# Attention over padded 128x128 tiles, products with queries on partitions, scaling moved to the eviction, long and short blocks in turn

## The chip, the cores and the metric

One Trainium2 chip, one core. The metric is the device time of one execution in microseconds (us), the median of the runs. TensorE (PE) multiplies, its weight loads are listed apart as PEld; VectorE is DVE, ScalarE is ACT, GpSimd is POOL, SyncE (SP) issues DMAs.

## What is computed

The whole program runs two recurrent mixer layers over 1024 tokens and then one transformer block. The change touches the attention of that block: for each of 8 query blocks of 128 tokens, a sliding-window attention with sinks (8 heads, 2 key-value heads) and a latent attention over the keys that an index picked (8 heads, keys and values the same 128 latent numbers). 16 meta tokens stand ahead of all others.

```
s  = einsum('bnqhgd,bnkhd->bnhgqk', qb, kw) * (64 ** -0.5) + bias      # window: own and previous block
pr = e / (e.sum(-1) + exp(sink - m));   o_a = einsum('bnhgqk,bnkhd->bnqhgd', pr, vw)
...
s  = einsum('bqhc,bqkc->bqhk', qa, c_sel) * scale + bias               # latent: selected keys only
pr = softmax(s);   lat = einsum('bqhk,bqkc->bqhc', pr, c_sel);   o_b = einsum('bphc,chd->bphd', lat, w_uv)
...
mixed = gate_a * (o_a @ w_branch_a) + gate_b * (o_b @ w_branch_b)
```

All data is float32. The profile shows two PE passes for such a product and one for a transpose.

## The kernel before, around the change

There is no scheduler. Each engine runs its own program, written out by hand, and waits on counters; `attend_order` is the one list that all engines follow in the attention, each doing its share of a step and skipping the rest. Query block i (0 to 7) has N = 144 + 128 i keys, in i + 2 key tiles: one of the 16 meta keys, the others of 128.

One step s_ carries a head k = s_ of the latent attention through a pipeline. PE does, in this order: `scores(s_)` (N columns, in pieces of at most 512), `latent(s_-3)` (probabilities times latents, a product for each key tile), `turn_p(s_-2)` (a transpose for each key tile, up to four to a bank), `raised(s_-4)` (latent result times w_uv). Between them DVE scales, masks and finds the row maximum (`scores`), ACT takes the exponentials (`expo`) and copies every PSUM result to SBUF, and POOL multiplies the exponentials by one over their sum (`scale`, line 2589), which `turn_p` waits for. Before, k runs through blocks 0, 0, ... 7, 7, eight heads each.

The window attention has 32 pieces m = s_ // 2 (block m // 4, a head of each key-value head). In an even step PE does `swa_scores(m)` and `swa_turn(m-1)`, in an odd step `swa_values(m-1)`. DVE and ACT make the softmax, POOL scales it (line 2583), and ACT copies the turned window, the event `pa` (line 1616), after the exponentials of `swa_scores(m)` (lines 1606 and 1607), as the list has them in that order. Every block also needs `queries` and `absorbed` (lines 1079 and 1089), two products that make the absorbed queries of its eight heads.

PE takes its PSUM banks in turn from rings, and waits until the bank's former tenant has been copied out. Nearly everything small shares one ring of two banks, 7 and 2:

```
swa_s, mla_s, mla_p, small_b = Ring([0], True), Ring([3, 4]), Ring([5, 6]), Ring([7, 2])
```

`small_b` serves `swa_turn`, `swa_values`, `queries`, `absorbed`, `latent` and `raised`. The PE lines of the profile are 1047 `swa_scores`, 1057 and 1058 `swa_turn`, 1069 and 1070 `swa_values`, 1079 `queries`, 1089 `absorbed`, 1097 `scores`, 1105 `turn_p`, 1113 `latent`, 1121 `raised`. When all is copied out (`attn_done`), SP issues the loads of the next stage.

## Time and profile before

| | us |
|---|---|
| time before, median of 3 runs | 3779.39 (3776.23 to 3781.73) |
| the profiled execution, its time | 3773.92 |
| its span | 3772.2 |
| PE busy in the span | 3529.2 (94%) |
| the attention stage, first transfer of PE work to last | 2417.6 to 2789.2 |
| in it: PE, DVE, ACT, POOL busy (2418 to 2794) | 356.1, 195.3, 212.7, 169.0 |

PE is busy 94% of the span, and 82% of the chain that ended last lies on it. The attention is a tenth of the span. A busy PE counts pipelined matmuls to their modelled ends, so the start of one group to the start of the next is the better measure of what it takes; the granted clock of a stretch (1.00 is 2.4 GHz, 0.50 is 1.2 GHz) stands in the tables by stretches. The profiled execution is 5.5 us under the median of the runs.

### The profile page before, as it was taken

The numbers are of one execution on the slowest core, as the hardware profiler recorded it, in microseconds if no ns is written. First come the engines' busy times: TensorE is split into PE (matmuls) and PEld (weight loads), VectorE is DVE, ScalarE is ACT, GpSimd is POOL, SyncE is SP. The second block draws the span as 40 slices with busy tenths as digits, with TensorE's granted clock in tenths as the row PEclk, the third lists the DMA queues.
The fourth block names the chain that finished last, engine by engine and source line by source line (L and its number), as shares of the span: only waits on it lengthen the run. The fifth ranks groups of instructions, "written<-read, shape, count | busy, mean of one in ns | idle before, by whom it ended". The sixth has DMA issues, their size and how long they took to land.

```text
span 3772.2 us, 46285 instructions
## 1 busy us (share of the span) xinstructions
PE 3529.2 (94%) x19030; PEld 2511.3 (67%) x19030; DVE 1698.5 (45%) x3307; ACT 1109.3 (29%) x2310; POOL 615.2 (16%) x872
## 2 busy tenths in 40 slices
PE   8889999989999899999878899899999999999997
PEld 7775876777677577577453344467754478888886
DVE  3433444344343435435417889656532232332424
ACT  3432442243244334133212111256531121111112
POOL 0210120011021423012511011235520000000000
PEclk9899999999999999999978999889999999999999
DMA  3010110110001011011010021100030011111111
GB/s 132 23 35 12 40 41 1 40 29 24 28 29 41 12 37 34 23 46 71 1 70 34 22 78 59 64 1 1 1 140 34 12 56 45 45 56 45 56 45 45
DMA packets 36527, 151.54 MB, mean 40 GB/s; under 512 B 4983, under 2 KB 9785, under 8 KB 28890
## 3 DMA queue, kind: packets, MB, share of 16 engines
q1 hardware_dynamic: 36314, 148.57, 11.4%
q8 instruction: 150, 2.46, 0.3%
q14 instruction: 63, 0.52, 0.0%
HBM read 132.82 MB, written 15.73 MB: 39 GB/s over the span
## 4 chain that ended last, share of the span: by engine, by line
PE 82%; DVE 7%; ACT 4%; POOL 3%; issue 2%; DMA 1%; SPq 0%; POOLq 0%; DVEq 0%; ACTq 0%
PE pp L540 7%; PE pp L541 7%; PE pp L542 7%; PE pp L1176 6%; PE pp L1178 6%; PE pp L1177 6%; PE pp L1026 6%; PE pp L706 5%; PE pp L1158 3%; PE pp L1113 2%; PE pp L1142 2%; PE pp L851 2%; PE pp L1016 2%; PE pp L1097 1%; PE pp L1002 1%
## 5 line engine op out<-in xcount | busy, mean ns | idle before, releaser
L540 PE MATMUL pp<-gx_hi,pw_hi 128*128 128x512 f32 x1168 | 485.9, 416 | 28.6 <-DVE pw_lo L1755 27.7
L541 PE MATMUL pp<-gx_lo,pw_hi 128*128 128x512 f32 x1168 | 466.1, 399 | 0.0
L542 PE MATMUL pp<-gx_hi,pw_lo 128*128 128x512 f32 x1168 | 465.9, 399 | 0.0
L540 PEld LDWEIGHTS pp<-gx_hi,pw_hi 128*128 128x128 f32 x1168 | 226.2, 194 | 77.1 <-DVE pw_lo L1755 30.5
L1176 PE MATMUL pp<-x_hi,wt_hi 128*128 128x512 f32 x704 | 274.7, 390 | 1.1 <-DVE x_lo L2289 1.1
L1178 PE MATMUL pp<-x_hi,wt_lo 128*128 128x512 f32 x704 | 274.2, 390 | 0.0
L1177 PE MATMUL pp<-x_lo,wt_hi 128*128 128x512 f32 x704 | 274.2, 389 | 0.0
L542 PEld LDWEIGHTS pp<-gx_hi,pw_lo 128*128 128x128 f32 x1168 | 225.3, 193 | 49.7
L541 PEld LDWEIGHTS pp<-gx_lo,pw_hi 128*128 128x128 f32 x1168 | 226.4, 194 | 43.6
L706 PE MATMUL pp<-xT,arena 128*128 128x512 f32 x512 | 233.8, 594 | 6.3 <-DVE arena L1929 6.3
L1755 DVE TENSOR_TENSOR pw_lo<-arena,pw_hi 128x1024 fp32r<-128x1024 f32 x73 | 89.5, 1228 | 242.0 <-ACT pw_hi L1231 241.9
L2331 DVE TENSOR_TENSOR arena<-arena,pp 128x1024 f32<-128x1024 f32 x22 | 26.9, 1222 | 375.0 <-ACT arena L1732 375.0
L1732 ACT ACTIVATE arena<-pp 128x1024 f32<-128x1024 f32 x22 | 22.6, 1029 | 556.8 <-PE pp L1178 556.8
L2188 DVE MAX8 small<-w 128x8 f32<-128x656 f32 (+6 forms) x180 | 167.1, 928 | 2.8
L2190 DVE MATCH_REPLACE8 w<-small,w 128x656 f32<-128x656 f32 (+6 forms) x180 | 164.4, 914 | 0.0
L2602 POOL TENSOR_SCALAR small<-small 128x1 f32<-128x1 f32 x16 | 3.0, 190 | 973.0 <-ACT arena L1687 973.0
L706 PEld LDWEIGHTS pp<-xT,arena 128*128 128x128 f32 x512 | 94.8, 191 | 94.1 <-issue 83.1
L1176 PEld LDWEIGHTS pp<-x_hi,wt_hi 128*128 128x128 f32 x704 | 132.2, 188 | 28.8 <-DVE x_lo L2289 1.4
L1177 PEld LDWEIGHTS pp<-x_lo,wt_hi 128*128 128x128 f32 x704 | 132.2, 188 | 27.6 <-issue 0.2
L1178 PEld LDWEIGHTS pp<-x_hi,wt_lo 128*128 128x128 f32 x704 | 132.2, 188 | 27.4
L1176 PE MATMUL pp<-wt_hi,a_hi 128*128 128x512 f32 x352 | 139.6, 397 | 4.7 <-DVE a_lo L2333 4.7
L2318 DVE TENSOR_TENSOR y<-y,pp 128x512 f32<-128x512 f32 x176 | 115.9, 685 | 60.6 <-PE pp L1178 60.0
(391 smaller groups left out, 6735.6 us busy)
## 6 DMA issues: line engine op xcount, KB each, us to landing
arena<-in_tiles_dram SPq DMA_DIRECT2D x73, 512.0 KB, 3.6
arena<-in_units_dram SPq DMA_DIRECT2D x33, 1024.0 KB, 4.9
xT<-in_w_outs_dram SPq DMA_DIRECT2D x6, 2048.0 KB, 8.4
xT<-in_wall_dram SPq DMA_DIRECT2D x6, 2048.0 KB, 8.2
w<-in_wall_dram SPq DMA_DIRECT2D x4, 2048.0 KB, 8.1
gates_scratch<-arena SPq DMA_DIRECT2D x32, 256.0 KB, 2.4
arena<-gates_scratch SPq DMA_DIRECT2D x8, 1024.0 KB, 4.9
arena<-in_xT_dram SPq DMA_DIRECT2D x8, 512.0 KB, 8.0
```

The lines of the kernel that those rows point to most:

```text
L540: mm(b[:, hs], wh[:, c], X[0][:, k, hs], k == 0, False)
L541: mm(b[:, hs], wh[:, c], X[1][:, k, hs], False, False)
L542: m = mm(b[:, hs], wl[:, c], X[0][:, k, hs], False, k == 7)
L706: m = mm(b, oT[:, t * 128:(t + 1) * 128], wo[:, t * 1024 + hf * 512:t * 1024 + hf * 512 + 512], t == 0, t == 3)
L1026: m = mm(b, xT[:, k, n * 128:(n + 1) * 128], ws[:, k * 512:(k + 1) * 512], k == 0, k == 7)
L1158: m = mm(b, mixT[n % 2][:, k * 128:(k + 1) * 128], wt[:, (k % 4) * 1024 + hf * 512:(k % 4) * 1024 + hf * 512 + 512], k == 0, k == 7)
L1176: mm(o, l[0][:, c], r[0][:, d], first, False)
L1177: mm(o, l[0][:, c], r[1][:, d], False, False)
L1178: return mm(o, l[1][:, c], r[0][:, d], False, last)
L2188: e.max(m8, wk[:, 0:N]).then_inc(*did("m8", i, r_))
L2190: e.match_replace(out=wk[:, 0:N], in_to_replace=m8, in_values=wk[:, 0:N], imm_value=MARK).then_inc(*did("mr", i, r_))
L2318: tt(yv, yv, at("dn", j, n, hf), ALU.add).then_inc(*did("yd", j, n, hf))
```

## The change

1. The tile of meta keys is padded: rows 16 to 127 of the values `ckv[:, 0, :]` and `av[:, 0, :]` are zero, and the first key tile is transposed, copied and multiplied as one of 128 (its other columns meet zeros). ACT's separate copy of 16 rows (line 1652) becomes part of the following one.
2. `raised` and `swa_values` have their operands exchanged: the result has queries on partitions, 64 columns wide, with the full array and 64 moving columns. So it is turned afterwards, several heads at a time: `turn_o` (two transposes for four heads of a latent block) and `swa_out` (two transposes for two window pieces), both in `small_b`.
3. Nothing is scaled on POOL. ACT multiplies by one over the sum when it copies `raised`, DVE when it copies `swa_values` (which ACT did before).
4. Blocks come in pairs: k even is a head of blocks 7, 6, 5, 4, k odd one of 0, 1, 2, 3. Both blocks' `queries` and `absorbed` of the first pair stand ahead of step 0, the later ones in steps 8, 9, 13 and 14 of 16. There is a third buffer for absorbed queries. The window's pieces keep their order.

```diff
-        qab = [a.rearrange("p (h c) -> p h c", h=8) for a in (room(1024), masks[:, :, :].rearrange("p l c -> p (l c)"))]
+        qab = [a.rearrange("p (h c) -> p h c", h=8) for a in (room(1024), masks[:, :, :].rearrange("p l c -> p (l c)"), room(1024))]
...
+        obq = [room(256), room(256)]
+        oaq = consts[:, 128:384]
...
+        def blk(q):
+            return q // 2 if q % 2 else 7 - q // 2
+
+        def step_of(i, hd):
+            return 16 * min(i, 7 - i) + 2 * hd + (i < 4)
+
+        def last_step(q):
+            return step_of(blk(q), 7)
+
         def keys(k):
-            i = k // 8
-            tiles = [(0, 0, 16)] + [(t_, 16 + 128 * (t_ - 1), 128) for t_ in range(1, i + 2)]
-            return (i, k % 8, Sb[k % 3], 144 + 128 * i, tiles, slice(i * 128, (i + 1) * 128))
-
-        def attend_order(queries, absorbed, scale, scores, latent, turn_p, raised, expo, swa_scores, swa_turn, swa_scale,
-                         swa_values):
-            queries(0)
-            absorbed(0)
-            for s_ in range(68):
+            q = k // 16 * 2 + k % 2
+            i = blk(q)
+            tiles = [(0, 0)] + [(t_, 16 + 128 * (t_ - 1)) for t_ in range(1, i + 2)]
+            return (i, k // 2 % 8, Sb[k % 3], 144 + 128 * i, tiles, slice(i * 128, (i + 1) * 128), qab[q % 3])
+
+        def attend_order(queries, absorbed, scale, scores, latent, turn_p, raised, turn_o, expo, swa_scores, swa_turn, swa_scale,
+                         swa_values, swa_out):
+            for q in range(2):
+                queries(q)
+                absorbed(q)
+            for s_ in range(69):
                 if 1 <= s_ < 65:
                     scale(s_ - 1)
                 if s_ < 64:
...
                     latent(s_ - 3)
                 if 2 <= s_ < 66:
                     turn_p(s_ - 2)
-                if s_ >= 4:
+                if 4 <= s_ < 68:
                     raised(s_ - 4)
+                if s_ >= 5 and (s_ - 5) // 2 % 4 == 3:
+                    turn_o(s_ - 5)
                 if s_ < 64:
                     expo(s_)
                 m = s_ // 2
...
                         swa_scores(m)
                     if 1 <= m < 33:
                         swa_turn(m - 1)
+                    if 3 <= m < 34 and m % 2:
+                        swa_out(m - 2)
                 else:
                     if m < 32:
                         swa_scale(m)
                     if 1 <= m < 33:
                         swa_values(m - 1)
-                i = s_ // 8 + 1
-                if i < 8 and s_ % 8 == 3:
-                    queries(i)
-                if i < 8 and s_ % 8 == 5:
-                    absorbed(i)
+                for later, at_ in ((2, 8), (3, 13)):
+                    q = s_ // 16 * 2 + later
+                    if q < 8 and s_ % 16 == at_:
+                        queries(q)
+                    if q < 8 and s_ % 16 == at_ + 1:
+                        absorbed(q)
...
-        attn_done = [("sv", 31), ("ra", 63), ("oa", 31), ("ob", 63), ("P", 63), ("sp", 31)]
+        attn_done = [("ot", 63), ("ao", 31), ("oT", 63), ("aT", 31), ("oa", 31)]
...
             def swa_values(m):
                 i, j, d, cs, k0, ln, bo = swa_keys(m)
                 pa = PA[d].rearrange("p (q t c) -> p q t c", q=2, t=2)
-                first = 128 if i else 16
                 b = place_(small_b, ("sv", m), ("oa", m))
                 pe.wait_ge(("pa", m))
                 for p in range(2):
                     r = slice(64 * p, 64 * p + 64)
-                    mm(b[r, 0:128], av[0:first, i, r], pa[0:first, p, 0, :], True, False)
-                    q = mm(b[r, 0:128], av[:, i + 1, r], pa[:, p, 1, :], False, True)
+                    for t_ in range(2):
+                        q = mm(b[:, r], pa[:, p, t_, :], av[:, i + t_, r], t_ == 0, t_ == 1)
                 q.then_inc(*did("sv", m))
 
+            def swa_out(m):
+                b = place_(small_b, ("ao", m), ("aT", m))
+                pe.wait_ge(("oa", m - 1), ("oa", m))
+                for t_ in range(2):
+                    q = tr(b[:, t_ * 128:(t_ + 1) * 128], oaq[:, t_ * 128:(t_ + 1) * 128], ident)
+                q.then_inc(*did("ao", m))
...
             def turn_p(k):
-                pe.wait_ge(("P", k))
+                pe.wait_ge(("x", k))
                 for q0 in range(0, len(some), 4):
                     b = place_(mla_p, ("tp", k, q0), ("pt", k, q0))
-                    for x_, (t_, a, c) in enumerate(some[q0:q0 + 4]):
-                        q = tr(b[0:c, x_ * 128:(x_ + 1) * 128], s_[:, a:a + c], ident)
+                    for x_, (t_, a) in enumerate(some[q0:q0 + 4]):
+                        q = tr(b[:, x_ * 128:(x_ + 1) * 128], s_[:, a:a + 128], ident)
                     q.then_inc(*did("tp", k, q0))
 
             def latent(k):
-                i, hd, s_, N, some, cs = keys(k)
+                i, hd, s_, N, some, cs, qa = keys(k)
                 b = place_(small_b, ("la", k), ("lat", k))
                 pe.wait_ge([("pt", k, q0) for q0 in range(0, len(some), 4)])
-                for t_, a, c in some:
-                    q = mm(b[:, 0:128], ckv[0:c, t_, :], PT[k % 2][0:c, t_, :], t_ == 0, t_ == i + 1)
+                for t_, a in some:
+                    q = mm(b[:, 0:128], ckv[:, t_, :], PT[k % 2][:, t_, :], t_ == 0, t_ == i + 1)
                 q.then_inc(*did("la", k))
 
             def raised(k):
-                i, hd, s_, N, some, cs = keys(k)
+                i, hd, s_, N, some, cs, qa = keys(k)
                 b = place_(small_b, ("ra", k), ("ob", k))
-                r = slice(64 * (k % 2), 64 * (k % 2) + 64)
                 pe.wait_ge(("lat", k))
-                mm(b[r, 0:128], wuv[:, hd * 64:(hd + 1) * 64], lat[k % 2], True, True).then_inc(*did("ra", k))
+                mm(b[:, 0:64], lat[k % 2], wuv[:, hd * 64:(hd + 1) * 64], True, True).then_inc(*did("ra", k))
+
+            def turn_o(k):
+                b = place_(small_b, ("ot", k), ("oT", k))
+                pe.wait_ge(("ob", k))
+                for t_ in range(2):
+                    q = tr(b[:, t_ * 128:(t_ + 1) * 128], obq[k % 2][:, t_ * 128:(t_ + 1) * 128], ident)
+                q.then_inc(*did("ot", k))
...
-                if i:
-                    act(PA[d], b, ACT.Copy).then_inc(*did("pa", m))
-                else:
-                    act(pa[0:16, :, 0, :], bb_[0:16, :, 0, :], ACT.Copy)
-                    act(pa[:, :, 1, :], bb_[:, :, 1, :], ACT.Copy).then_inc(*did("pa", m))
-
-            def swa_values(m):
+                act(PA[d], b, ACT.Copy).then_inc(*did("pa", m))
+
+            def swa_out(m):
                 i, j, d, cs, k0, ln, bo = swa_keys(m)
-                ac.wait_ge(("sv", m))
-                act(oaT[:, j, cs], at("sv", m)[:, 0:128], ACT.Copy).then_inc(*did("oa", m))
+                ac.wait_ge(("ao", m))
+                act(oaT[:, j - 1:j + 1, cs], at("ao", m)[:, 0:256].rearrange("p (t c) -> p t c", t=2), ACT.Copy
+                    ).then_inc(*did("aT", m))
...
                 for q0 in range(0, len(some), 4):
                     part = some[q0:q0 + 4]
                     b = at("tp", k, q0)
                     ac.wait_ge(("tp", k, q0))
-                    lo = 0
-                    if part[0][2] == 16:
-                        i_ = act(pt[0:16, 0, :], b[0:16, 0:128], ACT.Copy)
-                        lo = 1
-                    if lo < len(part):
-                        i_ = act(pt[:, q0 + lo:q0 + len(part), :].rearrange("p t q -> p (t q)"), b[:, lo * 128:len(part) * 128],
-                                 ACT.Copy)
-                    i_.then_inc(*did("pt", k, q0))
+                    act(pt[:, q0:q0 + len(part), :].rearrange("p t q -> p (t q)"), b[:, 0:len(part) * 128], ACT.Copy
+                        ).then_inc(*did("pt", k, q0))
 
...
             def raised(k):
-                r = slice(64 * (k % 2), 64 * (k % 2) + 64)
-                ac.wait_ge(("ra", k))
-                act(obT[r, hd // 2, cs], at("ra", k)[r, 0:128], ACT.Copy).then_inc(*did("ob", k))
+                ac.wait_ge(("ra", k), ("rd", k), ("ot", k - 2) if hd % 4 == 0 and k >= 2 else None)
+                act(obq[k % 2][:, hd % 4 * 64:hd % 4 * 64 + 64], at("ra", k)[:, 0:64], ACT.Copy, scale=mla_t[k % 6][2]
+                    ).then_inc(*did("ob", k))
+
+            def turn_o(k):
+                i, hd, s_, N, some, cs, qa = keys(k)
+                ac.wait_ge(("ot", k))
+                act(obT[:, hd // 4 * 2:hd // 4 * 2 + 2, cs], at("ot", k)[:, 0:256].rearrange("p (t c) -> p t c", t=2), ACT.Copy
+                    ).then_inc(*did("oT", k))
...
+            def swa_values(m):
+                j, rd = m % 4, swa_t[m % 2][5]
+                o = oaq[:, j % 2 * 128:j % 2 * 128 + 128]
+                dv.wait_ge(("sv", m), ("srd", m), ("ao", m // 2 * 2 - 1) if m >= 2 else None)
+                tt(o.rearrange("p (q c) -> p q c", q=2), at("sv", m)[:, 0:128].rearrange("p (q c) -> p q c", q=2),
+                   rd.unsqueeze(2).to_broadcast([128, 2, 64]), ALU.mult).then_inc(*did("oa", m))
...
+            e.memset(ckv[:, 0, :], 0.0)
+            e.memset(av[:, 0, :], 0.0).then_inc(*did("zpad"))
...
-            def swa_scale(m):
-                i, j, d, cs, k0, ln, bo = swa_keys(m)
-                rd = swa_t[d][5]
-                po.wait_ge(("srd", m))
-                for p in range(2):
-                    i_ = ts(sS[d][:, p, 0:ln], sS[d][:, p, 0:ln], rd[:, p:p + 1], None, ALU.mult)
-                i_.then_inc(*did("sp", m))
-
-            def scale(k):
-                i, hd, s_, N, some, cs = keys(k)
-                po.wait_ge(("rd", k))
-                ts(s_[:, 0:N], s_[:, 0:N], mla_t[k % 3][2], None, ALU.mult).then_inc(*did("P", k))
```

How PE's order moves is shown at two places. The first is an even step and the start of the odd one after it, in the middle of a sweep: PE before, from the window's scores in step 10 on (pp1 holds banks 2 and 3, pp3 banks 6 and 7; for `latent`, `raised`, the window's turn and values, pp3 is bank 7 and pp1 bank 2).

```order
L1047 MATMUL pp0<-arena 128x256 x2
L1057 MATMUL pp3<-consts,w2 128x128
L1058 MATMUL pp3<-consts,w2 128x128
L1057 MATMUL pp3<-consts,w2 128x128
L1058 MATMUL pp3<-consts,w2 128x128
L1097 MATMUL pp2<-arena,masks 128x272
L1113 MATMUL pp1<-arena 128x128 x3
L1105 MATMUL pp3<-consts,arena 16x128
L1105 MATMUL pp3<-consts,arena 128x128 x2
L1121 MATMUL pp3<-w3,xT 64x128
L1069 MATMUL pp1<-w2,arena 64x128
L1070 MATMUL pp1<-w2,arena 64x128
```

And PE now, from the window's scores in step 6 on (lines of the changed kernel: 1066 window scores, 1076 and 1077 window turn, 1095 `swa_out`, 1124 scores, 1140 `latent`, 1132 `turn_p`, 1147 `raised`, 1088 window values):

```order
L1066 MATMUL pp0<-arena 128x144 x2
L1076 MATMUL pp1<-consts,arena 128x128
L1077 MATMUL pp1<-consts,arena 128x128
L1076 MATMUL pp1<-consts,arena 128x128
L1077 MATMUL pp1<-consts,arena 128x128
L1095 MATMUL pp3<-consts 128x128 x2
L1124 MATMUL pp2<-arena,masks 128x144
L1140 MATMUL pp1<-arena 128x128 x9
L1132 MATMUL pp3<-consts,arena 128x128 x2
L1147 MATMUL pp3<-xT,w3 128x64
L1088 MATMUL pp1<-arena,w2 128x64 x4
```

Before, the bank of the window's turn (pp3) came back for `raised` (L1121), behind scores, `latent` and `turn_p`. Now, where `swa_out` stands behind the turn (m odd), that bank (pp1) comes back for `latent` (L1140), behind `swa_out` and the short block's scores alone. Where m is even there is no L1095, and the bank still comes back for `raised`.

The second place is the start of the stage on PE, before:

```order
L1079 MATMUL pp3<-arena,xT 128x128 x8
L1089 MATMUL pp1<-arena,xT 128x128 x4
L1089 MATMUL pp3<-arena,xT 128x128 x4
L1097 MATMUL pp1<-arena,w2 128x144
L1047 MATMUL pp0<-arena 128x144 x2
```

and now (1105 `queries`, 1115 `absorbed`):

```order
L1105 MATMUL pp3<-arena,xT 128x128 x8
L1115 MATMUL pp1<-arena,xT 128x128 x4
L1115 MATMUL pp3<-arena,xT 128x128 x4
L1105 MATMUL pp1<-arena,xT 128x128 x8
L1115 MATMUL pp3<-arena,xT 128x128 x4
L1115 MATMUL pp1<-arena,xT 128x128 x4
L1124 MATMUL pp1<-arena,w2 128x512
```

A second pair of `queries` and `absorbed` moved ahead of the first scores, and those are now of block 7.

## Rows read from the trace of the kernel before

**Rows 1.** The page: its first line.

```profile
span 3772.2 us, 46285 instructions
```

**Rows 2.** Stretches: length, busy PE, PEld, DVE, ACT, POOL, clock, DMA share, GB/s.

```profile
2424.30:2444.80 20.50, 18.55 (x71) 13.09 (x72) 8.80 (x35) 9.07 (x35) 5.21 (x8) 0.50 0.00 0
2448.20:2468.70 20.50, 20.50 (x76) 13.01 (x74) 6.39 (x21) 7.49 (x29) 3.19 (x5) 0.50 0.00 0
2478.90:2768.30 289.40, 275.81 (x1814) 198.50 (x1812) 169.38 (x436) 175.23 (x553) 147.31 (x104) 1.00 0.00 1
```

**Rows 3.** Timeline of PE, blocks 1 and 2: start, us, line, count, idle before.

```profile
2496.97 0.70 PE L1047 MATMUL pp<-arena 64*128 64x256 f32 x4
...
2498.65 1.12 PE L1113 MATMUL pp<-arena 16*128 16x128 f32 x6
2499.61 0.49 PE L1105 MATMUL pp<-consts,w 128*16 128x128 f32 x3
2501.35 0.43 PE L1121 MATMUL pp<-w,xT 128*64 128x128 f32 x2 [1.25 <-ACT w L1616]
...
2504.77 0.70 PE L1047 MATMUL pp<-arena 64*128 64x256 f32 x4
```

**Rows 4.** Timeline of DVE and ACT in the same pair of steps.

```profile
2497.72 0.69 DVE L2216 SCALAR_TENSOR_TENSOR w<-pp,arena 128x512 f32<-128x512 f32 x1 [0.95 <-PE pp L1047]
...
2499.63 0.51 ACT L1606 ACTIVATE w<-w,small 128x256 f32<-128x256 f32 x1 [1.73 <-DVE small L2224]
...
2500.73 0.57 ACT L1616 ACTIVATE w<-pp 128x512 f32<-128x512 f32 x1
```

**Rows 5.** Timeline of PE, block 4, two steps.

```profile
2595.02 0.32 PE L1121 MATMUL pp<-w,xT 128*64 128x128 f32 x1
...
2596.16 2.05 PE L1079 MATMUL pp<-arena,xT 128*128 128x128 f32 x16 [0.27 <-ACT xT L1667]
2598.05 1.27 PE L1097 MATMUL pp<-arena,w 128*128 128x512 f32 x4
2599.25 1.80 PE L1113 MATMUL pp<-arena 16*128 16x128 f32 x12
2600.88 0.82 PE L1105 MATMUL pp<-consts,w 128*16 128x128 f32 x6
2601.63 0.43 PE L1121 MATMUL pp<-w,xT 128*64 128x128 f32 x2
2601.99 0.49 PE L1047 MATMUL pp<-arena 64*128 64x256 f32 x2
```

**Rows 6.** Timeline of PE: block 7; last, an earlier stage.

```profile
2765.74 1.04 PE L1105 MATMUL pp<-consts,w 128*16 128x128 f32 x8
2767.07 0.33 PE L1105 MATMUL pp<-consts,w 128*128 128x128 f32 x1 [0.29 <-ACT arena L1655]
...
67.93 1.84 PE L566 MATMUL pp<-consts,arena 128*128 128x1 f32 x16
```

**Rows 7.** Stretches of the stage before, and a PE row of its timeline.

```profile
2076.20:2079.60 3.40, 1.25 (x6) 0.48 (x5) 0.88 (x2) 2.09 (x9) 0.02 (x1) 1.00 0.00 0
2079.60:2086.40 6.80, 6.80 (x9) 2.89 (x10) 5.96 (x12) 0.73 (x2) 1.47 (x4) 0.50 0.00 0
...
2093.13 1.18 PE L965 MATMUL pp<-arena 64*128 64x272 f32 x2 [2.15 <-DVE w L2166]
```

**Rows 8.** Timeline of PE, the start of the stage.

```profile
2417.59 3.62 PE L1079 MATMUL pp<-arena,xT 128*128 128x128 f32 x16 [5.65 <-DMA gates_scratch<-arena]
...
2424.37 0.85 PE L1097 MATMUL pp<-arena,w 128*128 128x144 f32 x2 [0.69 <-ACT w L1633]
```

**Rows 9.** Groups by shape in the attention; last, a piece of the chain behind.

```profile
L1652 ACT ACTIVATE arena<-pp 16x128 f32<-16x128 f32 x64 | 16.8, 262 | 7.7 <-PE pp L1105 6.5
...
L1105 PE MATMUL pp<-consts,w 128*16 128x128 f32 x43 | 12.3, 286 | 1.5 <-POOL w L2589 1.5
...
2793.14 25.43 DMA arena<-gates_scratch
```

More of the change, by code:

```diff
@@ L353, in program @@
         swa_t = [tuple(sm(2) for _ in range(6)) for _ in range(2)]
-        mla_t = [tuple(sm(1) for _ in range(3)) for _ in range(3)]
+        mla_t = [tuple(sm(1) for _ in range(3)) for _ in range(6)]
         def skewed(a):
@@ L1080, in queries, with absorbed @@
                                bqnT[:, kt, cs], kt == 0, kt == 1)
-                q.then_inc(*did("qu", i))
-            def absorbed(i):
-                pe.wait_ge(("quc", i))
+                q.then_inc(*did("qu", x))
+            def absorbed(x):
+                pe.wait_ge(("quc", x))
                 for odd in range(2):
-                    b = place_(small_b, ("ab", i, odd), ("qab", i, odd))
+                    b = place_(small_b, ("ab", x, odd), ("qab", x, odd))
                     r = slice(64 * odd, 64 * odd + 64)
@@ L1118, in raised @@
                 b = place_(small_b, ("ra", k), ("ob", k))
-                r = slice(64 * (k % 2), 64 * (k % 2) + 64)
                 pe.wait_ge(("lat", k))
-                mm(b[r, 0:128], wuv[:, hd * 64:(hd + 1) * 64], lat[k % 2], True, True).then_inc(*did("ra", k))
-            attend_order(queries, absorbed, skip, scores, latent, turn_p, raised, skip, swa_scores, swa_turn, skip, swa_values)
+                mm(b[:, 0:64], lat[k % 2], wuv[:, hd * 64:(hd + 1) * 64], True, True).then_inc(*did("ra", k))
@@ L1127, in did @@
+            def turn_o(k):
[4 more added lines that the diff above has]
+                q.then_inc(*did("ot", k))
+            attend_order(queries, absorbed, skip, scores, latent, turn_p, raised, turn_o, skip, swa_scores, swa_turn, skip,
+                         swa_values, swa_out)
             def did(*event):
@@ new lines, in swa_out, with queries, absorbed @@
+            def swa_out(m):
+                i, j, d, cs, k0, ln, bo = swa_keys(m)
+                ac.wait_ge(("ao", m))
+                act(oaT[:, j - 1:j + 1, cs], at("ao", m)[:, 0:256].rearrange("p (t c) -> p t c", t=2), ACT.Copy
+                    ).then_inc(*did("aT", m))
+            def queries(x):
+                ac.wait_ge(("qu", x), ("ab", x - 1, 1) if x else None)
+                act(qTb.rearrange("p t c -> p (t c)"), at("qu", x), ACT.Copy).then_inc(*did("quc", x))
+            def absorbed(x):
+                for odd in range(2):
+                    if x >= 3:
+                        ac.wait_ge(("sc", last_step(x - 3), chunks(144 + 128 * blk(x - 3))[-1][0]))
+                    ac.wait_ge(("ab", x, odd))
+                    act(qab[x % 3][:, odd:8:2, :], at("ab", x, odd).rearrange("p (h c) -> p h c", h=4), ACT.Copy
+                        ).then_inc(*did("qab", x, odd))
@@ L1663, in raised @@
             def raised(k):
[L1664 to L1669 removed]
+                i, hd, s_, N, some, cs, qa = keys(k)
+                ac.wait_ge(("ra", k), ("rd", k), ("ot", k - 2) if hd % 4 == 0 and k >= 2 else None)
+                act(obq[k % 2][:, hd % 4 * 64:hd % 4 * 64 + 64], at("ra", k)[:, 0:64], ACT.Copy, scale=mla_t[k % 6][2]
+                    ).then_inc(*did("ob", k))
+            def turn_o(k):
+                i, hd, s_, N, some, cs, qa = keys(k)
+                ac.wait_ge(("ot", k))
+                act(obT[:, hd // 4 * 2:hd // 4 * 2 + 2, cs], at("ot", k)[:, 0:256].rearrange("p (t c) -> p t c", t=2), ACT.Copy
+                    ).then_inc(*did("oT", k))
+            attend_order(queries, absorbed, skip, skip, latent, turn_p, raised, turn_o, expo, swa_scores, swa_turn, skip, skip,
+                         swa_out)
             def did(*event):
```

60 lines of the change are left out of this document (23 added, 37 removed).

## The prediction

> **What bounds the kernel now.** I read the page first: 3772.2 us of span [rows 1], most of it outside the attention and untouched. Then I cut the attention into stretches by the granted clock [rows 2]. From 2478.9 to 2768.3 the clock is full and PE is busy 275.8 of 289.4 us: PE bounds it, with short waits. Before that, while block 0's and 1's heads run, 20.5 us stretches go by at half clock. Next the timeline of PE in one pair of steps [rows 3]. From the window's scores (L1047, 2496.97) to the next ones (2504.77) a pair takes 7.80 us, and in it PE stands still ahead of `raised` (L1121, 2501.35) until ACT has copied the turned window (L1616). The other engines' timeline [rows 4] shows why so late: DVE starts on the window's scores at 2497.72, ACT has their bias at 2499.63, takes both exponentials, and only then, at 2500.73, copies the earlier window's turn. From L1047's start at 2496.97 to PE's resumption is 4.38 us; L1047 itself takes 0.54 of issue, so 3.84 us pass after it, and this chain consists of fixed pieces that do not depend on the block. `raised` needs that copy only because it gets the turn's bank in the ring of two. In long blocks PE has more to do than 3.84 us in between, and the wait vanishes. POOL is hardly waited for on PE: 1.5 us in the commonest shape [rows 9].
>
> **The change, part by part.** Passes first. Six passes of `latent` take 0.96 us with three tiles [rows 3], twelve 1.63 with six [rows 5]: 0.112 a pass, 0.223 a tile, and 0.29 fixed, which is the 16-row tile's. Another 0.09 stands ahead of it: `scores` of 656 columns takes 1.20 [rows 5], where 1.67 ns a column (PE's rate at full clock, two passes of two cycles) gives 1.10. Padding therefore gives back 0.38 x 64 = 24 us of PE work. A transpose is one pass of 0.109 the eight from 2765.74 in [rows 6]. `raised` in an even step takes 0.36 plus about 0.10 on the way in [rows 5], now two passes 0.22 and 0.09 on the way to the window's 64-row products: 0.15 x 32 = 5 us back. In an odd step `raised` and the window's values, which now share the array's column halves, take about 1.0 us 2595.02 to 2596.16 less the wait in [rows 5]; now ten passes. What does a pass with 64 moving columns and full weights cost? The trace has none, so bounds: by moving columns alone 0.054, by weight loads 0.111, since sixteen passes with a single moving column take 1.84 us, tail included [rows 6]. I take 0.111, the row that has such loads: 1.11, so 0.1 x 32 = 3 us lost. The Trainium skill ("TensorE: Matmul & The Clock Gate", Back-to-back issue gap) gives the isolated spacing by moving columns alone, and under "LDWEIGHTS (loading the stationary operand)" a load by its columns. By the first the sum would be 22 us lower; the one-column row goes with the second. The 64 new transposes cost 7 us. Work saved: about 19 us.
>
> ACT loses the 16-row copies (64 x 0.262 [rows 9]), DVE gains 32 small products; neither is full, so both count nothing, and if the cover were gone ACT's part is the 17 us at most. The memsets on POOL, unseen in the trace, lie between 0 and 1 us: 0.
>
> Now the order. A pair of steps has one long and one short head. PE's work in the even step up to the end of the window's scores is scores(long) + latent(short) + turns(long) + `raised` 0.22 + 0.09 + 0.54. In us, for blocks (7,0): 2.0 + 0.45 + 0.98 + 0.85, and 0.39 for the ninth turn, which waits for a bank as now [rows 6]: 4.67. (6,1): 3.92. (5,2): 3.82. (4,3): 3.72.
>
> With m even the bank of the window's turn comes back for `raised`, as before. PE reaches it after 0.53 + scores(short) + latent(long) + turns(short), 3.0 to 3.3 us, and waits 0.5 to 0.85. Pair: 4.67 + 3.84 + 0.22 + 0.89 = 9.6, then 8.9, 8.8, 8.7.
>
> With m odd, `swa_out` shifts the ring by one, and the bank comes back for **`latent` of the long head**. Ahead of that PE has only 0.53 + 0.22 + scores(short) 0.24 to 0.92. So PE stands still for 2.85, 2.6, 2.4 and 2.2 us, and queued behind the wait are latent(long), turns(short), `raised` and the values, which all come after: 4.67 + 3.84 + 2.01 + 0.22 + 1.16 = 11.9, then 11.0, 10.8, 10.6.
>
> Both kinds in all four groups, four times each: 321 us. The same way of adding gives 7.8 for the pair of [rows 3], where 7.80 stands.
>
> The six later blocks' queries cost 4.4 us each (sixteen passes of `queries`, 1.9 [rows 5], the rest `absorbed` with its switches): 26. `turn_o` with its bank waits: 7. The first two pairs lack their back part, while DVE and ACT handle block 7's first head in series: 16.2 us in place of 21.5, so -5. The drain from the last pair to the last `turn_o` copy, by ACT copies and products of blocks 4 and 3: 9. Start: before, L1079 at 2417.59 and scores at 2424.37 [rows 8]; now another queries (3.6, half clock, [rows 8]) and absorbed in between, with one copy each waited for, and the first scores at about 2430.1. Sum at full clock: 2430.1 + 321 + 26 + 7 - 5 + 9 = 2788. Before, the stage ended at about 2789.2, half-clock stretches included. So **the schedule alone returns nothing**: the 19 us of work and the POOL steps turn into waits, 15 of them long.
>
> **The clock.** Start and fill run at half clock: +6 over the figures above. Whether it recovers then is uncertain. If pair 2 runs at half as blocks 0 and 1 do [rows 2], +7 more. I take 7 in all, between 3 and 13. And the long waits: before the attention, PE was idle 2.15 us with the clock full (busy 1.25 of 3.4 us), and the 6.8 us behind it ran at half clock; a second idle time of 2.15 us is in the same stage [rows 7]. The waits of 1.25 us [rows 3] did not lower it [rows 2]. The new ones of 2.2 to 2.85 us are like the former. Such a fall of 6.8 us costs half of it, 3.4 us, where PE is the bound, and less where it waits anyway. I take six in ten of the 15 waits, at half of that, 1.7 us: 15 us; all of them at 3.4 would be 51, none 0.
>
> Sum: -1 + 7 + 15 = +21 us. Against the profiled execution, whose time is 3773.92, that is 3795; its median of runs stands 5.5 higher, at 3779.39, so I forecast 3800. The next stage's chain starts with its transfers (25.43 us [rows 9]) after the last copy and moves with it.
>
> **Rivals.** (a) *The clock holds.* Same waits, but the clock comes back by 2445 and the waits leave it: +3, so 3783. For it: the full clock held at PE busy 95% with short waits [rows 2]; against: rows 7. Chance 0.20.
>
> (b) *Faster: the bank wait does not bite.* It is one place, `latent` behind the bank of the window's turn with m odd. If the copy came before PE does, that is within 1.7 us of the window's scores in place of 3.84, odd pairs would be like even ones: 15 x 2.1 = 32 us less and no falls of the clock, 3753. It decides where the chain is shorter than what PE has in between. For it: ACT loses 17 us of copies. Against: the chain starts with DVE's two passes over 512 columns and the exponentials, which nothing shortens [rows 4]. Chance 0.11.
>
> (c) *A pass of 64 columns takes 0.054*: 320 passes of values and raised x 0.057, 22 us less with the even steps' raised, 3778. The skill's spacing by moving columns, named above, would have it so. Against: rows 6. Chance 0.06.
>
> (d) *The clock stays at half for long stretches* in the (7,0) and (6,1) groups: half clock stretches a pair of 11 by about 7; five such pairs, 3800 + 25 = 3825. For it: 20.5 us stretches twice [rows 2]. Chance 0.13.
>
> **How the numbers follow.** The forecast has 0.50, its own range 3787 to 3812 (start 3 to 13, falls 6 to 30, 0.1 us a pair). The 0.2% that a measurement tells from none is 7.6 us: same is 3772 to 3787. Slower: the forecast but 0.03, (d), and 0.04 of (a): 0.64. Same: 0.16 of (a), 0.03 of the forecast and (c), 0.06: 0.25. Faster: (b), 0.11. For 8 in 10 I leave out the far part of (b) and of (d): 3768 to 3822.
>
> **What would show it.** PE idle ahead of line 1140 with releaser ACT line 1647 (the turn's copy), some 15 times, 2 to 3 us each; ahead of line 1147 in even pairs 0.5 to 0.9. From one window score (line 1066) to the next 9.6 and 11.9 alternately in (7,0). `latent` of nine tiles 2.0 with no step after its first tile, line 1088's eight passes 0.89, no POOL. First scores at 2430, the stage's last copy near 2810. Clock at half in short pieces behind the long waits. The forecast is wrong if those waits are short, if line 1088 takes 0.45, or if the clock is full after 2445.

## The result

The changed kernel takes 3792.98 us (median of 6 runs, 3786.17 to 3796.3), the kernel before beside it 3779.91 (6 runs, 3776.23 to 3783.23): ratio 1.0032, 95% interval 1.0019 to 1.0045. It is 13 us **slower**; 3800 was forecast, and the time lies in the range. The profiled execution took 3794.53 us, 20.6 more than that of before. Of these, 7.3 lie ahead of the stage, in code that the change leaves alone but for two memsets and a wait for them, 11.2 in the attention (from its first product to the next stage's first: 371.2 us before, 382.4 now), 2.1 behind it. In the profiled executions of the kernels below the stage begins anywhere from 2411.0 to 2427.1, and both of these ends have the code of the kernel before ahead of the stage, so the 7.3 are not put down to the change. What the experiments below are about is the 11.2.

The page of the changed kernel, span and the busy times of part 1:

```profile
span 3792.8 us, 46132 instructions
PE 3517.5 (93%) x19094; PEld 2536.7 (67%) x19094; DVE 1708.1 (45%) x3339; ACT 1103.0 (29%) x2242; POOL 446.4 (12%) x746
```

POOL has nothing left in the attention. The waits of PE in the changed kernel from 2420 to 2820 (who waited for whom: us in total, times, longest):

```profile
PE pp L1140 <- ACT w L1647: 28.5, 15, 2.6
PE pp L1115 <- ACT w L1647: 8.6, 3, 2.9
...
PE pp L1147 <- ACT w L1647: 3.2, 7, 0.6
PE pp L1088 <- ACT w L1691: 2.4, 5, 0.6
PE pp L1124 <- DVE w L2280: 2.1, 1, 2.1
```

Line 1140 is `latent`, 1147 `raised`, 1115 `absorbed`, 1647 ScalarE's copy of the turned window. Waits for that copy hold more than all others together. Of the fifteen at `latent`, twelve take 1.88 to 2.62 us, each in a pair with m odd. Three short ones (1.06, 0.85 and 0.63) stand in pairs with m even, behind a block's `queries`, which there is the one more tenant of the ring (a tenant is the product that holds a bank). The three at `absorbed` take 2.87 each. In the same view of the kernel before, `raised` alone waits for the copy, and for shorter:

```profile
PE pp L1121 <- ACT w L1616: 7.1, 8, 1.3
```

One long wait of the changed kernel, blocks 4 and 3, in the timeline of PE:

```profile
2726.70 0.70 PE L1066 MATMUL pp<-arena 64*128 64x256 f32 x4
...
2727.72 0.27 PE L1077 MATMUL pp<-consts,arena 128*128 128x128 f32 x1
2727.82 0.38 PE L1095 MATMUL pp<-consts 128*128 128x128 f32 x2
2728.04 1.15 PE L1124 MATMUL pp<-arena,masks 128*128 128x512 f32 x4
2731.08 1.60 PE L1140 MATMUL pp<-arena 128*128 128x128 f32 x12 [1.89 <-ACT w L1647]
2732.52 0.71 PE L1132 MATMUL pp<-consts,w 128*128 128x128 f32 x5
2733.07 0.33 PE L1147 MATMUL pp<-xT,w 128*128 128x64 f32 x2
2733.24 0.39 PE L1153 MATMUL pp<-consts,w 128*128 128x128 f32 x2
...
2738.54 0.70 PE L1066 MATMUL pp<-arena 64*128 64x256 f32 x4
```

And the chain of work that ended last, in the same pair:

```profile
2726.77 0.66 PE pp L1066 x4
...
2727.45 0.70 DVE w L2248
...
2728.18 0.70 DVE small L2251
...
2729.36 1.09 ACT w L1640 x4
2730.45 0.09 ACT small L1641
2730.55 0.49 ACT w L1647
...
2731.08 1.60 PE pp L1140 x12
```

The copy (L1647) needs nothing of this pair's window scores: it reads the turn of the former pair's window, which PE has done by 2728 (L1077, 2727.72 + 0.27). It stands in ScalarE's order behind the exponentials (L1640) of *this* pair's window scores, and so behind VectorE's two passes. PE has `swa_out` and four short products of `scores` (L1095, L1124), then nothing. From the start of the window's scores to `latent` it is 4.38 us (2726.70 to 2731.08), as it was from L1047 to L1121 in [rows 3]. The prediction split the same 4.38 into 0.54 of issue and a chain of 3.84; the turn starts 0.63 us behind the scores in both traces, so the split is off by 0.09 us, and the 4.38, by which the pairs were summed, is not.

### The profile page after: what moved, and what is told of

Read it like the earlier page. It is cut to its first block, busy times and chain, and to the rows that moved or that the text cites. A ratio compares the mean times of both kernels' runs of the same rounds, so it can differ in the third digit from the quotient of the medians.

```text
span 3792.8 us, 46132 instructions
## 1 busy us (share of the span) xinstructions
PE 3517.5 (93%) x19094; PEld 2536.7 (67%) x19094; DVE 1708.1 (45%) x3339; ACT 1103.0 (29%) x2242; POOL 446.4 (12%) x746
## 4 chain that ended last, share of the span: by engine, by line
PE 82%; DVE 8%; ACT 4%; POOL 3%; issue 2%; DMA 1%; SPq 0%; POOLq 0%; DVEq 0%; ACTq 0%
PE pp L559 7%; PE pp L561 7%; PE pp L560 6%; PE pp L1210 6%; PE pp L1211 6%; PE pp L1212 6%; PE pp L1045 6%; PE pp L725 5%; PE pp L1192 3%; PE pp L1176 2%; PE pp L870 2%; PE pp L1140 2%; PE pp L1035 2%; PE pp L1124 1%; PE pp L917 1%
## 5 line engine op out<-in xcount | busy, mean ns | idle before, releaser
L559 PE MATMUL pp<-gx_hi,pw_hi 128*128 128x512 f32 x1168 | 486.6, 417 | 28.5 <-DVE pw_lo L1787 27.7
```

Of the source, the lines that this page charges most:

```text
L559: mm(b[:, hs], wh[:, c], X[0][:, k, hs], k == 0, False)
```

## Experiments

All kernels were timed beside the kernel before on the same chip; the ratio is to that one. "Stage" is the time from the attention's first product to the first of the next stage in the profiled execution.

| kernel | median us | before, same chip | ratio (95%) | stage | half clock in it |
|---|---|---|---|---|---|
| before | 3779.91 | | | 371.2 | 51.1 |
| changed | 3792.98 | 3779.91 | 1.0032 (1.0019 to 1.0045) | 382.4 | 41.5 |
| e2 out behind raised | 3763.82 | 3782.3 | 0.9945 (0.9927 to 0.9963) | 355.6 | 27.7 |
| e3 turn copied first | 3745.61 | 3782.3 | 0.9898 (0.9879 to 0.9917) | 338.0 | 21.0 |
| b3 before, turn copied first | 3769.18 | 3782.3 | 0.9958 (0.9941 to 0.9974) | 363.5 | 47.0 |
| e1 in sequence | 3781.67 | 3782.3 | 0.9995 (0.9982 to 1.0008) | 367.4 | 34.7 |
| b5 before, padded | 3742.62 | 3779.73 | 0.9894 (0.9876 to 0.9912) | 336.2 | 14.2 |
| b4 before, order alone | 3770.39 | 3779.73 | 0.9970 (0.9959 to 0.9982) | 361.8 | 30.8 |
| e13 in sequence, turn first | 3734.93 | 3779.73 | 0.9870 (0.9848 to 0.9892) | 328.2 | 10.8 |
| e23 both | 3739.26 | 3779.73 | 0.9885 (0.9864 to 0.9906) | 330.7 | 10.8 |
| b53 before, padded, turn first | 3735.96 | 3785.16 | 0.9875 (0.9863 to 0.9888) | 330.2 | 17.6 |
| b6 before, one more tenant | 3818.78 | 3785.16 | 1.0088 (1.0072 to 1.0104) | 407.9 | 84.4 |
| e123 all three | 3751.34 | 3785.16 | 0.9912 (0.9898 to 0.9927) | 337.5 | 14.2 |
| e7 out in the other ring | 3749.79 | 3775.34 | 0.9923 (0.9904 to 0.9942) | 344.4 | 14.2 |

### Is it the wait for the copy? (e2, e3, e7)

**e2** moves one tenant of the ring, in the common order of all engines:

```diff
                     if 1 <= m < 33:
                         swa_turn(m - 1)
-                    if 3 <= m < 34 and m % 2:
-                        swa_out(m - 2)
...
                 if s_ >= 5 and (s_ - 5) // 2 % 4 == 3:
                     turn_o(s_ - 5)
+                if s_ >= 7 and s_ % 4 == 3:
+                    swa_out(s_ // 2 - 2)
```

> The changed kernel, with swa_out taken out of the even steps and put behind raised and turn_o of every fourth odd step, one step later than before. Nothing else differs: same passes, same copies. The two-bank ring of the small results then has another sequence of tenants, and latent of an even step no longer follows the window turn's bank. Theory 1 (the wait of latent for ACT's copy of the turned window, 28.5 us over 15 pairs in the changed kernel's trace, is what the change lost): latent's wait on the window's copy is gone or below 5 us in all, the falls of the clock behind it (7, about 11 us) become few, and the time is 30 to 43 us under the changed kernel, 3750 to 3763, below the kernel before. Theory 2 (TensorE is held by its own work, and the wait only fills a slack that another wait would fill): another wait takes its place in the same pairs and the time moves by less than 8 us. Theory 3 (the order of long and short blocks costs): less than 8 us as well.

Measured 3763.82, 29 us under the changed kernel (33 by the ratios) and a microsecond above theory 1's range. The waits of its PE in the same stretch:

```profile
PE pp L1147 <- ACT w L1647: 6.6, 14, 0.6
PE pp L1115 <- ACT w L1647: 6.0, 3, 2.0
PE pp L1140 <- ACT w L1647: 2.5, 3, 1.1
```

`latent` waits 2.5 us where it waited 28.5 (only its three short waits are left), and `raised`, which stands behind `latent` and the turns, 6.6. The three waits at `absorbed` stay, with 2.0 us each: they come with the new order, as b4 shows below.

**e3** leaves PE's and VectorE's order and the ring alone, and exchanges two things for ScalarE, whose program alone passes `turn_first=True`:

```diff
                 if s_ % 2 == 0:
+                    if turn_first and 1 <= m < 33:
+                        swa_turn(m - 1)
                     if m < 32:
                         swa_scores(m)
-                    if 1 <= m < 33:
+                    if not turn_first and 1 <= m < 33:
                         swa_turn(m - 1)
```

> The changed kernel, with one exchange in ScalarE's order: in an even step it copies the turned window of the pair before ahead of the two window exponentials, not behind them. TensorE's and VectorE's orders stay as they are, so the ring's tenants too. Theory 1 (latent waits 1.9 to 2.6 us because the copy stands behind two exponentials that themselves wait for this pair's window scores): the chain from the turn to the copy shrinks from about 3.8 to about 1.5 us, all waits for that copy (28.5 + 8.6 + 3.2 us in the changed kernel's trace) go below 8 us, the clock stays full behind them, 3740 to 3760. Theory 2 (another wait takes its place): the exponentials start about 0.8 us later, so VectorE's row sums and the window turn of the next pair come later; the time moves by less than 8 us, and the chain of waits names the window's scale or the exponentials.

Measured 3745.61, 47 us less; the forecast of theory 1 was 3740 to 3760. A pair like the one above, in the timelines of PE and ACT of e3 (`latent` is line 1142, the copy 1649 here):

```profile
2690.46 0.38 PE L1097 MATMUL pp<-consts 128*128 128x128 f32 x2
2690.68 1.15 PE L1126 MATMUL pp<-arena,masks 128*128 128x512 f32 x4
2691.68 1.58 PE L1142 MATMUL pp<-arena 128*128 128x128 f32 x12
...
2690.83 0.61 ACT L1649 ACTIVATE w<-pp 128x512 f32<-128x512 f32 x1
2691.99 0.51 ACT L1642 ACTIVATE w<-w,small 128x256 f32<-128x256 f32 x1 [0.55 <-DVE small L2258]
```

The copy starts at 2690.83, as soon as ScalarE is done with the exponentials of the latent head, and `latent` follows `scores` without a gap. In the changed kernel 1.89 us of nothing stood between the two.

**e7** separates the ring from the place in the order: one word, with every engine's instructions where they were.

```diff
-                b = place_(small_b, ("ao", m), ("aT", m))
+                b = place_(mla_p, ("ao", m), ("aT", m))
```

> The changed kernel with its instructions in their order, and one word changed: the turned window output takes a bank of the ring of the turned probabilities (mla_p) and not of the small ring. Theory 1 (the count of tenants in the small ring between the window's turn and latent is what makes latent wait): with that tenant gone from it, latent's wait on the window's copy is gone, as when the output's turn was moved behind raised (3764); raised, behind turn_p, keeps a short one of about 0.5 us; 3755 to 3770. The next turn_p's bank may now wait for ScalarE's copy of the output, which would show there. Theory 2 (moving the output's turn to the odd step helped by its place in ScalarE's order, not by the bank): 3785 or more.

Measured 3749.79, ratio 0.9923: 41 us under the changed kernel by the ratios, and 5 us below the range that I gave. So it is the *count* of tenants between the window's turn and `latent` that matters, not where the turn of the output stands; at the other ring no wait of note came up (1.1 us in all, 4 times).

### The same wait put into the kernel before (b6, b3)

**b6** adds to the kernel before one transpose of the identity matrix, in every second pair behind the window's turn. Nobody reads it, so it only takes a bank's turn (its output is part of no result):

```diff
+                    if one_more and 3 <= m < 34 and m % 2:
+                        one_more(m - 2)
...
+            def one_more(m):
+                b = place_(small_b, ("om", m), ("om", m))
+                tr(b[:, 0:128], ident, ident).then_inc(*did("om", m))
```

> The kernel before with one more tenant of the two-bank ring in every second pair: a single transpose of the identity matrix, that nobody reads, behind the window's turn, where the changed kernel has its window's output turn. Nothing else is changed; it adds 16 passes of 0.11 us, under 2 us. Theory 1 (the order of tenants decides which product meets the window's bank): latent, ahead of turn_p, waits for the copy instead of raised, behind it; each wait is longer by the turns that stood between (0.6 to 1.1 us), 15 times, 9 to 16 us, and falls of the clock come on top: 3792 to 3810. Theory 2 (the added products and the turned layout cost in the changed kernel, the ring's order does not): within 4 us of the kernel before, 3777 to 3785.

Measured 3818.78, ratio 1.0088: 33.6 us lost for 16 passes of 0.11 us, 9 us more than theory 1 had at most. The pair of blocks 4 of which the kernel before has a piece in [rows 5] begins in b6's timeline of PE so (line 1119 is `latent`):

```profile
2604.40 0.70 PE L1049 MATMUL pp<-arena 64*128 64x256 f32 x4
...
2605.53 0.27 PE L1065 MATMUL pp<-consts 128*128 128x128 f32 x1
2605.64 1.27 PE L1103 MATMUL pp<-arena,w 128*128 128x512 f32 x4
2608.78 1.79 PE L1119 MATMUL pp<-arena 16*128 16x128 f32 x12 [1.88 <-ACT w L1623]
...
2618.13 0.70 PE L1049 MATMUL pp<-arena 64*128 64x256 f32 x4
```

This pair takes 13.73 us, 11.67 in the kernel before (from 2590.32 to the last row of [rows 5]). The pairs without the extra tenant keep their length to 0.02 us at full clock (7.90, 8.55, 11.35, 9.01, 12.23). My expectation of 0.6 to 1.1 us a wait was too low: not only the turns but `latent` itself stood ahead of the old wait at `raised`, and so in the copy's cover. Waits are not all of it: the stage has 33 us more at half clock than that of the kernel before (84.4 for 51.1).

**b3** is e3's exchange in the kernel before.

> The kernel before with the same exchange in ScalarE's order (the copy of the turned window ahead of the window's exponentials). It is the control of the run with this exchange in the changed kernel. Theory 1: in the kernel before the ring's tenants let latent pass without that wait in nearly all pairs (its waits of 1.25 us and less stand at the window's turn and at raised), so the exchange gives little: 0 to -12 us, 3768 to 3780, and more in the changed kernel by at least 20 us. Theory 2 (the exchange helps either order alike, because ScalarE is what sets a pair): both kernels gain the same within 8 us.

Measured 3769.18: 13 us gained (16 by the ratio), against 47 in the changed kernel. Theory 1 holds: the exchange is worth much more where the bank comes back for `latent`.

### The parts by themselves (b5, b4, e1, e13)

**b5** pads the meta tile in the kernel before: `tiles = [(0, 0, 128)] + ...`, full-height turns and products, the memsets, and one ScalarE copy a bank.

> The kernel before with the padding alone: the 16 meta keys' tile is turned and multiplied as 128 rows (the 112 rows behind them are zero in the keys and values), and ScalarE copies such a bank in one instruction. Blocks in sequence, products and scaling as before. By the prediction's first term (0.38 us for each of the 64 heads where a 16-row tile stands between 128-row tiles) TensorE loses 24 us of work, a few of them where it waits anyway: 3752 to 3765. A rival, that the change of tile costs nothing by itself and the 0.38 us are a wait that shows up elsewhere: within 5 us of the kernel before.

Measured 3742.62, 37 us less and 9 us under my range. The work term is right. The stretch of [rows 5] in b5's timeline of PE:

```profile
2577.99 1.27 PE L1096 MATMUL pp<-arena,w 128*128 128x512 f32 x4
2579.10 1.50 PE L1112 MATMUL pp<-arena 128*128 128x128 f32 x12
2580.44 0.82 PE L1104 MATMUL pp<-consts,w 128*128 128x128 f32 x6
```

`scores` to `latent` 1.11 us for 1.20, `latent` to the turns 1.34 for 1.63: 0.38 a head, as summed. But in pairs that the chain holds it becomes a wait (`raised` waits 16.7 us for the copy in b5), so the 24 pairs from the eighth on give only 13.7 us. The rest comes from the first seven pairs: 71.8 us in the kernel before, 52.0 in b5. Two stretches of b5 show why:

```profile
2428.70:2438.90 10.20, 8.40 (x40) 6.39 (x39) 7.03 (x30) 6.42 (x24) 5.10 (x8) 0.50 0.00 1
2438.90:2757.60 318.70, 294.81 (x2106) 226.81 (x2105) 188.67 (x498) 200.50 (x589) 164.07 (x121) 1.00 0.00 1
```

The clock is back at full by 2438.9, 10.7 us after the first scores, and stays there to the end. In the kernel before it is at half for two stretches of 20.5 us, with PE busy 90% and 100% of them [rows 2], and for a third, shorter one. Why it came back in one and not in the other was not tested by itself; the height of the tiles is the only difference in PE's work, and ScalarE has fewer copies.

**b4** has the order alone in the kernel before (`blk`, `step_of`, queries of two blocks up front, three buffers for them).

> The kernel before with the new order alone: long and short blocks in turn, queries and absorbed two blocks ahead, three buffers of absorbed queries. 16-row tiles, key-major last products, GpSimd's scaling and the tenants of the ring between two window turns are as before. Theory 1 (the order by itself is nearly free: it ends 9 us later in its drain and starts 4 us later, and spares the long half clock of the short blocks at the start): 3770 to 3790. Theory 3 (the order is what costs, the sequence run of the changed kernel being 11 us faster): 3791 or more. Theory 4 (it is what saves): 3765 or less.

Measured 3770.39, at the lower end of theory 1's range. Its PE waits for the window's copy at `absorbed` three times, 2.15 us each, without any `swa_out`: of the 8.6 us that the changed kernel waits there, 6.4 come with the order. **e1** undoes the order alone in the changed kernel:

```diff
-            return q // 2 if q % 2 else 7 - q // 2
+            return q
...
-            q = k // 16 * 2 + k % 2
+            q = k // 8
             i = blk(q)
```

> The changed kernel with its blocks one after the other (0 to 7) and everything else kept: padding, queries on partitions, turned outputs, scaling at eviction. It says what the turn of long and short blocks is worth by itself. Theory 1 (the order is worth little, the loss sits in the bank wait, which every second pair has in either order): the bank wait shows up in about as many pairs, a little longer in long blocks, where ScalarE's exponentials are longer; time within -10 to +12 us of the changed kernel, 3783 to 3805. Theory 3 (mixing long with short blocks is what cost): at least 10 us under the changed kernel, about the time of the kernel before or less. Theory 4 (the mixing covers short blocks' waits and is what saved the change from worse): over 15 us above the changed kernel, with the half clock over most of the short blocks.

Measured 3781.67, ratio 0.9995: 11 us under the changed kernel, 14 by the ratios. That is a microsecond past theory 1's range and inside theory 3's (at least 10 us under the changed kernel), so by the time alone the order costs here; by the ratios it gains 11 us in the kernel before and loses 14 in the changed one. In sequence `latent` still waits 25.0 us in 15 places, so that wait does not hang on the order, and theory 3 does not account for it.

**e13** is e1 with e3's exchange.

> The changed kernel with its blocks in sequence and the copy of the turned window ahead of the window's exponentials in ScalarE's order. With the wait for that copy gone it says what the order of the blocks is worth by itself. If the 11 us by which the changed kernel in sequence was faster came out of the order (later first scores, longer drain), this run is 5 to 15 us below the changed kernel with the copy first (3746): 3731 to 3741. If they came from the wait, which falls in 15 pairs of unequal slack and brings falls of the clock, both are within 5 us: 3741 to 3751. If short blocks alone are held by ScalarE and VectorE and the mixing covers that, it is above 3752.

Measured 3734.93, ratio 0.9870, 11 us under e3 (3745.61). So in the changed kernel without its long wait the order still costs about 11 us. Part of it is read from the traces: e13 has 10.2 us less at half clock (10.8 for 21.0), worth 5.1 us at most, and e3 waits 4.5 us at `absorbed` for copies of the window and of its output, which e13 does not, though e13 waits elsewhere (5.3 us at the window's values for 2.7). The later first scores (10.7 us behind the first queries in place of 6.9) are mostly work that is moved and not added. What the remainder is was not separated.

### Is there anything left? (e23, b53, e123)

> The changed kernel with both edits: the window's outputs turned behind raised in every fourth odd step, and the copy of the turned window ahead of the window's exponentials. If both edits remove the same wait, little is left for the second: within 5 us of the copy first alone (3746), 3741 to 3751. If they remove different ones, their gains (29 and 47 us) add up: 3715 to 3735.

Measured 3739.26, 2 us below the range of the first case and 4 above that of the second: nearly all that both edits remove is the same wait.

> The kernel before with the padding and with the copy of the turned window ahead of the window's exponentials; sequence, key-major last products and GpSimd's scaling as before. Set beside the changed kernel in sequence with the same copy first (3735), it says what queries on partitions, the turned outputs and the scaling at eviction are worth with the wait for the copy gone. Raised waits 16.7 us for that copy in the padded kernel, so I expect 3722 to 3728. If the prediction's sum for these parts holds (TensorE has 5 us more work for them), the distance to 3735 is 3 to 10 us. A rival, that these parts save time once the wait is gone (GpSimd is out of the path): 3740 or more.

Measured 3735.96, 8 to 14 us above what I expected; the gain over b5 is 7 us and not 17. The wait at `raised` went, and one at the window's values came: its bank's last tenant is `latent`, whose copy (L1650) stands in ScalarE's order behind the window's exponentials too:

```profile
PE pp L1070 <- ACT w L1650: 7.8, 10, 1.3
```

> The changed kernel with all three edits: blocks in sequence, the copy of the turned window first, and the window's outputs turned behind raised. The copy first removed nearly all waits in sequence (5.3 us for the output copies are left), so 3728 to 3737, within 6 us of the two edits alone (3735). Above 3742 it would show that the place of the output turn costs in sequence.

Measured 3751.34, 14 us above the range: in sequence the output's turn behind `raised` brings waits of its own, at the window's values (L1089) and at that turn (L1096). The first of these rows stands in e13 too (5.3 us, 6 times), the other two are new but for 0.2 us:

```profile
PE pp L1089 <- ACT w L1687: 5.3, 6, 1.5
PE pp L1089 <- ACT w L1692: 5.1, 12, 0.6
PE pp L1096 <- ACT w L1687: 4.5, 5, 1.1
```

So the place that helped in one order hurt in the other. e13 (0.9870), b53 (0.9875) and e23 (0.9885) are the best and not told apart by their intervals; each is 1.1 to 1.3% below the kernel before.

## Why the prediction was right

**The wait: right.** It was to stand at `latent` of the long head, 15 times, 2.2 to 2.85 us. Twelve stand there, 1.88 to 2.62 us, each 0.2 to 0.3 us shorter than set (one, in (7,0), 0.9), and the other three at `absorbed`, 2.87 us, because in step 14 of 16 `absorbed` inherits the bank. That the prediction had not worked out, nor the three short waits behind `queries`, 2.5 us in all. Such a place in the timeline of PE:

```profile
2613.02 0.38 PE L1095 MATMUL pp<-consts 128*128 128x128 f32 x2
2616.27 2.82 PE L1115 MATMUL pp<-arena,xT 64*128 64x128 f32 x16 [2.87 <-ACT w L1647]
```

e3, e7 and b6 show the wait as the cause, from both sides. The 4.38 us from the window's scores are there to the hundredth.

**The pairs: right to 0.2 us, but for one group.** From window score to window score at full clock, even m: 8.9 and 8.7 for (6,1) where 8.9 was summed, 8.6 to 8.8 (8.8) for (5,2), 8.5 to 8.7 (8.7) for (4,3). Odd m: 11.13 (11.0), 10.84 (10.8); the pair shown, 11.84, has two `turn_o` and a bank wait in it, about 1 us that the sum holds apart (10.6). In (7,0) an even pair takes 9.06 where 9.6 was summed. The waits of `raised`, set at 0.5 to 0.85 in every even pair, are 3.2 us in all, 7 times, 0.6 at most.

**A pass of 64 columns: right.** Eight passes of the window's values, L1088, in the timeline of PE, up to the next line:

```profile
2722.84 1.06 PE L1088 MATMUL pp<-arena,w 128*128 128x64 f32 x8
2723.73 1.32 PE L1124 MATMUL pp<-arena,w 128*128 128x512 f32 x4
```

0.89 us, 0.111 a pass at full clock: rival (c), with 0.054, is out. The Trainium skill ("TensorE: Matmul & The Clock Gate", LDWEIGHTS (loading the stationary operand)) has the load's time go by its columns, 128 / 1.2 = 107 ns; the trace agrees within 5%.

**Padding's work: right as work (0.38 a head, b5).** What I did not see is its other half, that most of the early half clock goes with it (19.8 us of the first seven pairs in b5, of which the work is the smaller part). In my sum this gain was contained only because I counted the new stage at full clock against an old one that ended with its half-clock stretches included. Nor is it sure that padding earned it there: the order alone (b4, 16-row tiles) has 10.3 us at half clock in its first 25 us and full clock for the next 75.

**Last products with queries on partitions: not refuted.** Summed at about 5 us of added work; e13 and b53, which differ in these parts and in POOL's scaling alone, are 1 us apart, with e13 the faster. Their intervals (0.9848 to 0.9892 and 0.9863 to 0.9888) hold 5 us more as well, and each has waits of its own, so the term is not shown. That POOL's end in the stage earned next to nothing fits its 1.5 us of waits in [rows 9]; it was not timed by itself.

**Start and fill at half clock: too dear.** The term was 7 us, 3 to 13. First scores come 10.7 us behind the first product where I had 12.5. One fall of 6.8 us came in the fill, 0.6 us behind a wait of 2.07 us for VectorE (the first head's scores), and then the clock is full over most of the second and third pair:

```profile
2449.80:2470.30 20.50, 18.03 (x126) 14.25 (x125) 12.49 (x39) 11.85 (x39) 0.00 (x0) 0.99 0.00 0
```

**Falls behind the long waits: right in kind, a little too dear.** I had taken nine at 1.7 us, 15 us. Seven came, each within 2 us of the end of a long wait (four at `latent`, three at `absorbed`); five lasted 3.4 us, and two 6.8, in the stretches:

```profile
2617.10:2623.90 6.80, 6.80 (x36) 6.34 (x35) 1.54 (x5) 1.43 (x3) 0.00 (x0) 0.53 0.00 0
2753.60:2760.40 6.80, 6.80 (x29) 5.77 (x28) 2.47 (x6) 1.68 (x5) 0.00 (x0) 0.53 0.00 0
```

Eight long waits of 1.88 to 2.42 us had none. I estimate the cost of the seven at about 11.5 us in all. Only two pairs can be set beside a like one or its sum: the one with the second of these rows takes 13.93 us where 10.6 was summed, the one at 2543 takes 13.29 against 12.10 at 2589.

Together: the stage was to grow by 21 us and grew by 11.2; start and falls, 22 in the sum, came to about 14 if the rest of the sum holds (371.6 us from the first scores to the next stage, less the 358 summed at full clock), and the first scores are 1.8 us earlier. The medians' 13 us go with it. Rival (a), the clock holding, gave 3783 (by its own terms, 3779.4 - 1 + 3, it is 3781) and is out in its cause, since the clock did fall; the time lies between it and the forecast. Rival (b) is out: the wait bites. Rival (d) is out: no stretch of the stage at half clock is longer than 6.8 us.

## What to carry to other kernels

Where several kinds of results share a ring of PSUM banks, one more tenant shifts who inherits whose bank. List for each product the tenant before it, and when the engine that empties that bank gets to it *in its own order*: a copy that needs nothing new should not stand behind work that waits for this step's result. And time a change's parts apart: here the padding alone was worth 37 us, one tenant in the wrong ring cost 41 and the order, in this kernel, 11 to 14, and what showed was 13 us lost.

## What was not expected of the hardware

The kernel before, with its 16-row tiles, ran 51 us of this stage at half clock; with those tiles padded to 128 rows and nothing else changed for PE it was 14 us, although each of them holds more rows. In b6, where PE stands still up to 2.5 us in most of the odd pairs, it was 84 us, most of it in the first eight pairs. Small terms thus had a second price at the start of the stage, where the clock had not yet risen; what of the tiles or the waits sets it, these runs do not separate. Height alone does not: with 16-row tiles and the long blocks first (b4) the start had 10.3 us at half clock. Nor does a fall need a long wait: in the kernel before two followed waits of 0.74 and 1.01 us, and b3 and b53 each have one of 3.4 us ahead of which PE waited nowhere as long as 0.5 us.
